# Four tiles of the second modulation move under the first mixer's output projection

## The reference

```python
# first block
x = x + 0.5 * g0 * swiglu(h, w13[0], w2[0])       # first FFN
y = hybrid_mixer(h, ...)                          # ends with: merged @ w_out
x = x + mod[:, 1, 2][:, None, :] * y              # the first mixer's update of x
x = x + 0.5 * g2 * swiglu(h, w13[1], w2[1])       # second FFN
# second block
mod = (jax.nn.silu(c) @ ada_w[i] + ada_b[i])[:, None, :]      # 1024 -> 6 * 1024
mod_c = jax.nn.silu(c_ctx) @ ada_w[i][:, :2 * D_MODEL] + ada_b[i][:2 * D_MODEL]
hn_ctx = modulate_2(rms_norm_2(h_ctx, norm1_g[i]), mods_c[0], mods_c[1])
hn_lat = modulate_2(rms_norm_2(h_lat, norm1_g[i]), sh1, sc1)
```

## Time and profile before

| | us |
|---|---|
| median of 3 runs | 1704.76 (1704.52 to 1706.03) |
| profiled execution, device time | 1707.38 |
| profiled execution, span from first to last instruction | 1705.6 |
| TensorE busy in the span | 1681.9 |
| VectorE / ScalarE / GpSimd busy | 1145.5 / 690.2 / 67.4 |

### The profile page before, as it was taken

The page is one execution under the profiler, slowest core; times in us unless marked ns, Lnnn a source line. Parts: engine busy times, 40 slices in busy tenths (PEclk is TensorE's granted clock), DMA queues, the critical chain, the costliest instruction groups (busy, mean ns, idle before and its releaser), DMA issues.

```text
span 1705.6 us, 24579 instructions
## 1 busy us (share of the span) xinstructions
PE 1681.9 (99%) x8956; PEld 1408.0 (83%) x8956; DVE 1145.5 (67%) x2122; ACT 690.2 (40%) x1048; POOL 67.4 (4%) x56
## 2 busy tenths in 40 slices
PE   7999999999999999999999999999999999999998
PEld 5788888888878868897888888888868988989897
DVE  3778578655655686469969973469675558656563
ACT  4421222234236573354222334342466443626262
POOL 0000000011000000200000000200000200000002
PEclk9999999999999999999999999999999999999999
DMA  9866567332523302537666642354200232434231
GB/s 330 259 203 197 178 201 212 108 103 54 145 74 98 99 1 75 171 106 219 188 205 188 175 116 80 112 169 113 87 1 15 86 112 74 119 85 124 85 108 50
DMA packets 355674, 218.59 MB, mean 128 GB/s; under 512 B 8544, under 2 KB 353668, under 8 KB 355588
## 3 DMA queue, kind: packets, MB, share of 16 engines
q1 hardware_dynamic: 355356, 217.37, 43.8%
q10 hardware_dynamic: 232, 0.09, 0.0%
HBM read 215.34 MB, written 2.11 MB: 127 GB/s over the span
## 4 chain that ended last, share of the span: by engine, by line
PE 95%; DVE 2%; DMA 1%; issue 1%; ACT 0%; SPq 0%; POOL 0%; DVEq 0%; ACTq 0%; POOLq 0%
PE bank L777 24%; PE bank L779 24%; PE bank L778 24%; PE bank L1314 2%; PE bank L1315 2%; PE bank L1313 2%; PE bank L1039 2%; PE bank L1023 1%; PE bank L955 1%; PE bank L959 1%; PE bank L956 1%; PE bank L1101 1%; PE bank L1273 1%; PE bank L1075 1%; DMA GBUF<-in_w_ada 1%
## 5 line engine op out<-in xcount | busy, mean ns | idle before, releaser
L1471 ACT ACTIVATE W_HI<-RAW 128x1024 fp32r<-128x1024 f32 x278 | 292.3, 1056 | 463.2 <-PE bank L779 401.5
L777 PE MATMUL bank<-H_HI,W_HI 128*128 128x512 f32 x1090 | 426.1, 391 | 3.9 <-DVE W_LO L1955 3.8
L778 PE MATMUL bank<-H_LO,W_HI 128*128 128x512 f32 x1090 | 424.7, 390 | 0.0
L779 PE MATMUL bank<-H_HI,W_LO 128*128 128x512 f32 x1090 | 424.7, 390 | 0.0
L1955 DVE TENSOR_TENSOR W_LO<-RAW,W_HI 128x1024 fp32r<-128x1024 f32 x254 | 311.3, 1226 | 95.3 <-ACT W_HI L1471 92.1
L777 PE MATMUL bank<-A_HI,W_HI 128*128 128x512 f32 x714 | 279.7, 392 | 0.0
L778 PE MATMUL bank<-A_LO,W_HI 128*128 128x512 f32 x714 | 278.2, 390 | 0.0
L779 PE MATMUL bank<-A_HI,W_LO 128*128 128x512 f32 x714 | 278.2, 390 | 0.0
L777 PEld LDWEIGHTS bank<-H_HI,W_HI 128*128 128x128 f32 x1090 | 204.7, 188 | 49.3 <-issue 5.1
L779 PEld LDWEIGHTS bank<-H_HI,W_LO 128*128 128x128 f32 x1090 | 204.7, 188 | 42.4
L778 PEld LDWEIGHTS bank<-H_LO,W_HI 128*128 128x128 f32 x1090 | 204.8, 188 | 42.2 <-issue 0.2
(11 more groups left out here) (435 smaller groups left out, 2313.5 us busy)
## 6 DMA issues: line engine op xcount, KB each, us to landing
RAW<-in_ffn_w SPq DMA_DIRECT2D x116, 512.0 KB, 4.8
GBUF<-in_w_ada SPq DMA_DIRECT2D x32, 1024.0 KB, 7.4
RAW<-in_mlp_w SPq DMA_DIRECT2D x64, 512.0 KB, 4.1
RAW<-in_w_in SPq DMA_DIRECT2D x57, 512.0 KB, 3.9
GBUF<-in_ada_w SPq DMA_DIRECT2D x24, 1024.0 KB, 7.2
RAW<-in_w_out SPq DMA_DIRECT2D x16, 512.0 KB, 4.0
RAW<-in_ffn_w SPq DMA_DIRECT2D x16, 384.0 KB, 3.4
PBUF<-in_w_ada SPq DMA_DIRECT2D x4, 1024.0 KB, 10.9
```

What stands on the lines that cost most here:

```text
L777: pe.matmul(dst, w_hi, x_hi, start=first and i == 0, stop=False)
L778: pe.matmul(dst, w_hi, x_lo, start=False, stop=False)
L779: mm = pe.matmul(dst, w_lo, x_hi, start=False, stop=last and i == len(blocks) - 1)
L1471: act.activation(strip_of(W_HI, slot), strip_of(RAW, slot), ACT.Copy).then_inc(hi_ready, 1)
```

## The change

Four of the 24 tiles, those of `gem_down1(1)`, are no longer summed in the down projection of the second FFN's second part, but in the first mixer's output projection. `GEM_OUT = (0, 0, 3, 4)` places them: two after the split at j = 0 and ahead of the wait for strip 0's products and so of the first update of X, one after the update of strip 3 and one after that of strip 4. SyncE loads the four tiles between strips 6 and 7 of `w_out`, behind the wait for the eighth `mlo_ready`, which stood after strip 7. Its loop over the eight strips is written out. The tiles' sequence numbers in the second FFN shift by four. The down projection of the second part, now without tiles, runs as a loop of two turns of four strips on VectorE, as the third part's does.

```diff
         GEM_PLAN = [[...],
-                    [(8, gem_up1(0), 4, gem_down1(0)), (8, gem_up1(1), 4, gem_down1(1)), (0, None, 0, None)]]
+                    [(8, gem_up1(0), 4, gem_down1(0)), (8, gem_up1(1), 0, None), (0, None, 0, None)]]
+        GEM_OUT = (0, 0, 3, 4)
...
-            load_strips(U_OUT, KC, lambda m: w_out[:, :, bass.ds(m * P, P)])
-
-            sp.wait_ge(mlo_ready, KC)
+            for m in range(KC):
+                load_strip(U_OUT + m, (U_OUT + m) % RING, w_out[:, :, m * P:(m + 1) * P])
+                if m == KC - 2:
+                    sp.wait_ge(mlo_ready, KC)
+                    for g in range(GEM_RING):
+                        load_gem_after(g, T_ADA + g, ada2(gem_down1(1)(0, g)))
+
             sp.dma_start(CTOK[:, :].rearrange("p (t d) -> p t d", t=2),
                          a["ctx_2"][0].rearrange("(t p) d -> p t d", p=P)).then_inc(ctx_in, 16)
-            load_ffn(U_FFN1, 1, T_ADA, w13[1], w2[1], ada2)
+            load_ffn(U_FFN1, 1, T_ADA + GEM_RING, w13[1], w2[1], ada2)
...
                         split_next(u0, it, j)
+                        if u0 == U_OUT and j == 0:
+                            for g in range(2):
+                                gem_step(g, seq_no + g, vec, tile(0, g))
                         dve.wait_ge(strip_done, it * RING + (u0 + j + 1 + RING))
                         dve.scalar_tensor_tensor(out=chunk(X, it * RING + j), ...)
...
-                        if j in gem_at:
+                        if j in gem_at and (u0 != U_OUT or j):
                             g = gem_at.index(j)
                             gem_step(g, seq_no + g, vec, tile(0, g))
...
-                down(U_OUT, MOD, 40, halves=True)
+                down(U_OUT, MOD, 40, T_ADA, C_2, gem_down1(1), GEM_OUT, halves=True)
...
-            ffn(U_FFN1, 1, T_ADA, C_2, 2 * KC, C_CTX, [...], [...])
+            ffn(U_FFN1, 1, T_ADA + GEM_RING, C_2, 2 * KC, C_CTX, [...], [...])
```

More of the change, by code:

```diff
@@ L2703, in _ @@
             norm_halves(A_1 + 2 * KC, 48, U_OUT + KC, MOD, 40)
-            ffn(U_FFN1, 1, T_ADA, C_2, 2 * KC, C_CTX, [last_gate, context_rms, second_modulation], [nothing, context, nothing])
+            ffn(U_FFN1, 1, T_ADA + GEM_RING, C_2, 2 * KC, C_CTX, [last_gate, context_rms, second_modulation], [nothing, context, nothing])
             mixer2()
```

## The result

| kernel | median | lowest to highest | span of the profiled run |
|---|---|---|---|
| before, on the same chip | 1704.69 us | 1704.45 to 1708.18 | 1705.6 us |
| changed | 1706.50 us | 1706.13 to 1711.26 | 1704.5 us |

The ratio is 1.0012, with a 95% interval of 1.0007 to 1.0018: +1.8 us (1.2 to 3.1). Forecast were 1706.4 us.

The account below looks back on a forecast made before the run. TensorE, busy 1681.9 of 1705.6 us, was taken to bound the kernel. +1.95 for later tiles, 0 for early tiles and transfers, -0.3 at the context made +1.6: median 1706.4 us, range 1704.0 to 1708.6.

Parts of the forecast that it names:

- The gain at the context: End of the second FFN's second down projection: waits at fold and transposes go without the four tiles, 0.3 us gained.
- The 0.09 us at the fold: Context's fold: it could start at 1001.26 instead of 1001.35 once the wait for FOLDED goes, 0.09 us.
- The loads: SyncE, output projection: four 1 MB transfers ahead of strip 7, first landing 5.1 us after issue, cost 0.
- The two early tiles: Output projection, ahead of the first update: strip 4's split ready at 708.6, 2.0 us of cover left, cost 0.
- The two later tiles: Output projection, among later updates: GpSimd's additions interrupt the tiles, token sums start at 733.2 instead of 731.24, cost 1.95 us.
- each turn: Later tiles: each GpSimd addition let in between VectorE's sums holds the tile up by 1.15 us.
- case A: Later tiles: VectorE keeps the port pair through a tile, they cost 0 to 0.3 us, 1704.5 in all; chance 0.33.
- The sum: Whole kernel: +1.95 for the later tiles, 0 for early tiles and transfers, -0.3 at the context, +1.6 us.
- the relief: Second FFN's second part: taking the four tiles out of its down projection gains 0.3 us.
- rival C: TensorE: the stop lowers its clock to 1.2 GHz for a few us, +2 to +4 us on top; chance 0.04.

Follow-up runs that it names:

- e3: Changed kernel with all four loads and waits, but VectorE writes zeros instead of summing these four tiles: 1704.41 us.
- e4: Changed kernel with the four tile loads issued behind strip 7 and CTOK instead of ahead of them: 1712.47 us.
- e1: Changed kernel with only the two early tiles moved; the other two go back to the second part's down projection: 1704.45 us.
- e5: Changed kernel with three tiles instead of two ahead of the first update of x, and one among the later ones: 1708.91 us.
- e2: Changed kernel with the first six of GpSimd's seven SSUM additions cut from 512 to 8 columns: 1704.41 us.
- e6: Kernel before, with two tiles (three sums) of the second FFN's first turn moved under the output projection instead of the four: 1702.57 us.

## Why the prediction was right

**The gain at the context: 0.3 forecast, 0.2 measured.** The 0.22 us of the transposes went, as said: from their start to the next matmul 1.93 us before (1001.54 to 1003.47) and 1.72 after (1000.59 to 1002.31). The 0.09 us at the fold did not. Before, the 0.35 us ahead of the fold was put down to FOLDED; after, with FOLDED long done, it is the same 0.35 and put down to issue. From the last matmul to the fold's first it is 0.32 us in both. I had taken the pace of like matmuls, 0.227 us, for the time that a change of operands takes. The releaser named beside an idle time needn't be its cause.

**The loads: cost 0, right.** The first tile starts at 697.97 on the clock of before (forecast 698.1), 5.2 us after its issue; e3 shows that the transfers are free, e4 what they would have cost later.

**The two early tiles: cost 0, right.** Update 0 at 706.76 (forecast 706.7), split of strip 4 ready at 708.63 (708.6). That this fits so closely is in part luck: a tile with another tile right behind it takes 4.49 us, not 4.29, and the first one landed 0.1 earlier than forecast. e1 shows no cost, and e5's delay of 2.49 us behind a third tile of 4.49 that the cover was 2.0.

**The two later tiles: 1.95 forecast.** By its steps, on the clock of before: third tile from 713.69 to 719.40 (forecast 713.6 to 719.5), fourth from 721.19 to 726.53 (721.3 to 726.7), last split ends 731.77 (731.95), half update 731.70 (731.9), last addition ends 732.90 (733.1), token sums 733.01 (733.2). The third tile takes 5.71 us, 0.38 for the addition already under way and 1.03 for one let in; the fourth takes 5.34, 1.05 for one let in. I had put each turn at 1.15, from the one pair of rows where W_LO and an addition meet; a tile pays 1.03 to 1.05. The sums take turns with the additions instruction by instruction: case A, that VectorE keeps the ports through a tile, is out for these two tiles (in e2 it happened once, see below). Together that is 2.46 us within tiles, and the half update is 1.70 late: without these turns it would be in time, as it is in e2. The last split, 1.66 in place of 1.23, has a turn only because it is late.

The Trainium skill (SBUF — State Buffer, section "SBUF: two separate sides") says that the port pair that VectorE and GpSimd share is held by one of them for a whole instruction. The third and the fourth tile agree with it: an addition got in, and the six sums together took 1.03 and 1.04 us more than 2.46.

**The sum.** In the traces: +1.77 at the token sums, 1.87 one step later in the norm, -0.2 at the context, +1.7 in all; in medians +1.8; forecast +1.6. Two small errors of the same size nearly cancel: 0.1 too much for the turns and 0.1 too much for the relief. What remains between 1.7 and 1.8 is less than the runs can tell.

**What the prediction had too low** is the chance of rival C, 0.04. It judged by a stop like the one of before (1.25 us), behind which the clock stays. In e5 a stop 0.7 us longer than the one made here was followed by the lower clock. The price it gave, 2 to 4 us, was on the other hand too high: in e5 it was 1.74 us. Three of the changed kernel's twenty runs took 1710.8 to 1711.3 us, and none of before's more than 1708.2. The 2.8 us of a start at the lower clock, and 1.7 us behind the stop at the token sums, would add up to that; no profile shows such a run, and it stays open.

## What to carry to other kernels

Idle time of an engine is worth something only up to where the next engine in line waits for it: add up the idle time, take off the wait for the first transfer and the work that is moved in, and see who stands behind the rest. Here 21 us of idle time took 17 us of tiles and a wait of 4, and the 2.5 us in which another engine's additions held the tiles up were already too much; e6 put in three tile sums in place of four, kept 2 us, and gained 2.1. Move into a gap what makes something else late: the four tiles of the change cost 0.2 us where they were, two others cost 2.1 us where they were.

A tile of VectorE paid about 1 us here for every GpSimd addition of 1.3 us that came due during it, so count those beside the tile's own time. And before a stop of TensorE is priced by its length alone, look at the granted clock behind it.

## What the runs showed of the hardware that I had not expected

**The clock behind a stop.** In the changed kernel, idle times of 1.26 us (behind the matmul at 775.07) and 1.61 us (the token sums) left the granted clock at 1.00, with TensorE busy for 0.58 of 2 us in the latter's window; so did 1.83 us at the token sums of e4. Idle times of 2.33 us (e5) and 4.22 us (e4) were followed by 0.43 us a matmul for some 3 us:

```profile
728.00:730.00 2.00, 0.58 (x5) 0.38 (x4) 1.35 (x2) 1.83 (x4) 1.88 (x1) 1.00 0.65 180
```

```profile
712.00:714.00 2.00, 1.87 (x4) 1.49 (x5) 2.00 (x3) 1.79 (x3) 1.73 (x2) 0.50 0.19 52
```

(the first is of the changed kernel, the second of e4). And the same stop may do the one or the other: between 20 and 22 us TensorE was busy for 0.82 us in the execution of before and for 0.83 in that of the changed kernel, and the clock fell in the first and not in the second (the first windows above).

**GpSimd isn't always let in at once.** In the changed kernel, e4 and e6 the additions that came due in a tile's sums ran through in 1.30 to 1.32 us, in e5 the one in 1.50. In e2 the fourth one, of only 8 columns, began within the sums of the third tile and took 2.21 us, to 712.86, just when the six sums had ended at 712.81; the next one, in the fourth tile, took 0.24 (timeline of GpSimd):

```profile
710.65 2.21 POOL L760 TENSOR_TENSOR SSUM<-SSUM,SQ 128x8 f32<-128x8 f32 x1 [1.35 <-ACT SQ L1488]
716.74 0.24 POOL L760 TENSOR_TENSOR SSUM<-SSUM,SQ 128x8 f32<-128x8 f32 x1 [3.87 <-ACT SQ L1488]
```

So GpSimd usually gets in between two back-to-back operations of VectorE here, but not always. What decides it wasn't settled. And it isn't only the operations with two tiles as inputs that are held up: the third tile's products (0.99 for 0.62 us) read one tile, GBUF, and a column of scalars, CSIL.

**SyncE is held by a full queue.** The timeline of SyncE in the changed kernel: the four tile loads' instructions take 5.35 us together (the fourth alone 2.82), that of strip 7 2.92 and that of CTOK 3.11. That is about what 1 MB takes at 350 GB/s, as if each had to wait until the transfers ahead had made room; no run tests that:

```profile
689.90 5.35 SPq L574 DMA_DIRECT2D GBUF<-in_ada_w  x4
695.29 2.92 SPq L570 DMA_DIRECT2D RAW<-in_w_out  x1
698.25 3.11 SPq L693 DMA_DIRECT2D CTOK<-in_ctx  x1
```

CTOK landed 10.3 us after its issue. Here nobody asks for it before 958 us; a load behind CTOK could be issued only at 701.36, 11 us after the first tile load.
